# Combining expert results by diagonal matmuls tile by tile, with column norms, and a different gather and scatter distance

## The chip, the core and the metric

The program runs on one core of a Trainium2 chip. The metric is device time in microseconds (us). A core has TensorE (PE; PEld is its weight load), VectorE (DVE), ScalarE (ACT), GpSimd (POOL) and SyncE (SP); the last three start DMAs here. SBUF and PSUM have 128 partitions; PSUM has eight banks of 512 fp32 columns.

## The reference

One inference step of a two-layer trunk on 512 latent and 128 context tokens of width 1024, all in fp32. Layer 0 mixes by attention and retention, layer 1 by a convolution module; each is followed by a mixture of 32 experts of which every token uses two. Cut to the parts that the change touches:

```python
def rms_norm(x, g):
    y = x * lax.rsqrt(jnp.mean(x * x, axis=-1, keepdims=True) + EPS)
    return y * g

def conformer_conv(h, w_in, dw, dw_b, ln_g, ln_b, w_out):
    a, g = jnp.split(h @ w_in, 2, axis=-1)
    u = depthwise_conv(a * jax.nn.sigmoid(g), dw, dw_b)
    u = layer_norm(u, ln_g, ln_b)
    return jax.nn.silu(u) @ w_out

# grouped_expert_mlp, after rows are gathered by expert
def run(args):
    xb, e = args
    a, b = jnp.split(xb @ w_up[e], 2, axis=-1)
    return (jax.nn.silu(a) * b) @ w_down[e]
out_buf = lax.map(run, (x_buf, blk_exp)).reshape(P, D)
y = out_buf[dest].reshape(N, TOP_K, D) * top_w[..., None]
return jnp.sum(y, axis=1)          # x = x + gate * this
```

## The kernel before

Every engine has its own instruction stream, written out by hand. Semaphores named by `ev(...)` join them, and an engine waits in program order. There is no scheduler. Activations lie transposed: `xT` and `hT` hold 8 tiles of 128 features by 640 tokens, that is 5 token tiles of 128, the last being the context.

**Order of the work.** Layer 0 mixer, `project_out` (L589), norm, router and ranks, block loop over experts, combine; layer 1 norm, gated input (L1029), convolution taps (L1046 on PE, L1960 on DVE), layer norm, `project_out`, norm, router, block loop, combine, transposes out (L1080), output DMAs (L529).

**Block loop.** Tokens are sorted by expert into blocks of 64 rows. SP streams 3 MB of weights for each expert into 18 slots of 1 MB, six experts deep (`refill`, L473 and L476). POOL gathers a block's rows into one of four landing buffers (L2114) and scatters a result block to `y_rows` in HBM (L2119). Gathers go two blocks ahead, scatters four blocks behind; the last four scatters stand in a tail behind the loop, each after a wait for the one before it (`freed`). PE transposes rows (L930), multiplies up (L945) and down (L967); DVE takes landed rows (L1884) and the gated product; ACT copies a result block out of PSUM (L1388). The number of blocks is rounded up to a multiple of four.

**Combine.** POOL's `y_done` (L2177) lets ACT start five DMAs of 1 MB that bring each token tile's two results back, 128 tokens by 2 by 1024 (L1404). ACT scales the first by its weight (L1409), DVE adds the second times its weight (L1913), PE transposes (L1009), and DVE adds the result times the gate to `xT` (L1922).

**Norms.** `norm_sums` (L563, L564) or `norm_sum` (L571, L572) multiplies squares by a matrix of ones, so that every partition holds the sums of all 640 tokens. ACT takes the roots (L1178, L1179), DVE the reciprocals (L1485, L1486), DVE multiplies (L1456) and ACT scales and shifts (L1184). The layer norm does the same with L1054 and L1980.

Lines by name:

```python
    dve.wait_ge(ev("comb"), 2 * NT)     # all five tiles combined
    normed(2)                           # the norm ahead of layer 1
    link(dve.reciprocal(PS[:, 4, :], rs[:, 0:SAMPLE]))
```

## Time and profile before

| what | value |
|---|---|
| median of 3 runs | 1504.81 us (1500.93 to 1506.77) |
| the profiled execution's own time | 1506.75 us |
| its span in the profile | 1504.9 us |
| mean granted clock of TensorE | 0.929 of 2.4 GHz |
| busy PE / DVE / ACT / POOL | 83% / 40% / 21% / 20% |
| DMA, mean over the span | 214 GB/s |

Durations below are from the one profiled execution. 1.85 us of its time lie outside the span. PE's busy share is an average over stages with different limits, so the rows further down are read stage by stage. One fp32 matmul of the program appears as two PE instructions, a transpose as one. The two block loops run from 544.6 to 791.3 us and from 1213.5 to 1461.5 us. A timeline row reads: start, duration, engine, line, operation, output <- input, count, and in brackets the idle time before it and what ended that.

### The profile page before, as it was taken

Reading aid. Unit: us, or ns where it says so; the run is one execution under the profiler, and the core shown is the slowest. Engines: PE = TensorE matmul, PEld = TensorE weight load, DVE = VectorE, ACT = ScalarE, POOL = GpSimd, SP = SyncE. Lnnn points to the kernel's source line nnn. Section 1 sums busy time; section 2 is a strip of 40 time slices with the busy share of each in tenths; the row PEclk is TensorE's granted clock in tenths of the full one; section 3 lists DMA queues with packets and bytes.
Section 4 is the critical chain, followed back from the end, with each engine's and each line's share of the span. In section 5 each row is a group of like instructions: output and inputs, shape, how many; then the busy total and the mean of one; then the engine's idle time right before and its main releaser. Section 6 shows DMA issues by size and latency. Waiting matters only on the chain.

```text
span 1504.9 us, 20559 instructions
## 1 busy us (share of the span) xinstructions
PE 1254.5 (83%) x6795; PEld 779.2 (52%) x6796; DVE 601.5 (40%) x1364; ACT 310.2 (21%) x666; POOL 304.0 (20%) x703
## 2 busy tenths in 40 slices
PE   4999998888899669997771699999798679999764
PEld 3666775554467335543330367776475345555333
DVE  1211433765421632221111569999612622222115
ACT  3300145655300411111111300000311311111112
POOL 3000100300000024443332012240000034444420
PEclk9999999979999769999995699999899779999996
DMA  9575646300061169999999010100071279999965
GB/s 341 218 277 233 267 169 243 129 31 1 1 252 56 70 230 402 412 406 402 398 359 349 4 56 29 56 29 1 0 274 62 97 270 396 385 402 409 405 248 208
DMA packets 149091, 322.60 MB, mean 214 GB/s; under 512 B 16181, under 2 KB 49947, under 8 KB 142883
## 3 DMA queue, kind: packets, MB, share of 16 engines
q1 hardware_dynamic: 128432, 288.25, 50.3%
q0 software_dynamic: 12464, 21.91, 4.1%
q10 hardware_dynamic: 8131, 11.57, 2.1%
q8 instruction: 42, 0.69, 0.2%
q14 instruction: 22, 0.18, 0.0%
HBM read 312.41 MB, written 27.08 MB: 226 GB/s over the span
## 4 chain that ended last, share of the span: by engine, by line
PE 48%; DVE 16%; SPq 14%; DMA 8%; issue 7%; ACT 3%; POOL 2%; ACTq 1%; POOLq 0%; DVEq 0%
PE PS L589 10%; PE PS L638 8%; DVE arena L1960 8%; SPq L476 7%; PE PS L945 7%; SPq L473 5%; PE PS L967 3%; DMA ring<-in_moe_w_up 3%; PE PS L555 3%; PE PS L1029 2%; PE PS L812 2%; DMA arena<-y_rows 2%; DVE scratch L1456 2%; PE PS L1046 2%; PE PS L827 1%
## 5 line engine op out<-in xcount | busy, mean ns | idle before, releaser
L589 PE MATMUL PS<-arena,ring 128*128 128x320 f32 x512 | 144.1, 446 | 11.1 <-ACT arena L1435 7.4
L945 PE MATMUL PS<-arena 128*64 128x256 f32 x1152 | 134.7, 383 | 21.5 <-DMA arena<-in_moe_w_up 20.6
L1456 DVE TENSOR_TENSOR arena<-arena,PS 128x128 f32<-128x128 f32 (+1 forms) x85 | 27.1, 327 | 311.0 <-ACT arena L1377 304.7
L1960 DVE SCALAR_TENSOR_TENSOR arena<-arena,vecT 128x655 f32<-128x655 f32 x181 | 151.1, 908 | 0.0
L945 PE MATMUL PS<-ring,arena 128*64 128x256 f32 x1056 | 129.0, 395 | 23.2 <-DMA ring<-in_moe_w_up 21.6
L1029 PE MATMUL PS<-arena,ring 128*128 128x320 f32 x512 | 141.2, 437 | 8.3 <-ACT arena L1184 7.2
L638 PE MATMUL PS<-ring,arena 128*128 128x256 f32 (+1 forms) x640 | 140.3, 373 | 0.0
L589 PEld LDWEIGHTS PS<-arena,ring 128*128 128x128 f32 x512 | 100.6, 197 | 54.3 <-issue 15.7
L638 PEld LDWEIGHTS PS<-ring,arena 128*128 128x128 f32 x640 | 114.9, 190 | 26.5 <-issue 13.4
L1029 PEld LDWEIGHTS PS<-arena,ring 128*128 128x128 f32 x512 | 98.4, 193 | 49.9 <-issue 10.1
L945 PEld LDWEIGHTS PS<-arena 128*64 128x64 f32 x1152 | 80.2, 137 | 64.9 <-DMA arena<-in_moe_w_up 17.3
L945 PEld LDWEIGHTS PS<-ring,arena 128*64 128x64 f32 x1056 | 76.2, 141 | 66.3 <-DMA ring<-in_moe_w_up 19.1
L1377 ACT ACTIVATE arena<-PS 128x128 f32<-128x128 f32 x69 | 19.1, 277 | 275.6 <-PE PS L945 275.6
L2009 POOL TENSOR_SCALAR arena<-arena,modA,modT 128x128 f32<-128x128 f32 x24 | 10.7, 447 | 300.6 <-DVE arena L1456 300.6
L967 PE MATMUL PS<-arena 128*64 128x512 f32 x288 | 69.8, 605 | 1.5 <-ACT arena L1388 1.5
L2119 POOL DMA_INDIRECT y_rows<-arena,scatter_col x64 | 65.1, 1017 | 22.1 <-issue 22.1
L1388 ACT ACTIVATE arena<-PS 128x512 f32 x61 | 36.4, 597 | 147.3 <-PE PS L967 147.3
L1009 PE MATMUL PS<-cst,arena 128*128 128x128 f32 x80 | 19.4, 415 | 56.4 <-DVE arena L1913 43.1
L2114 POOL DMA_INDIRECT arena<-h_rows,gather_col x56 | 59.3, 1059 | 28.3 <-issue 28.3
L1743 DVE SCALAR_TENSOR_TENSOR xT<-PS,modT,xT 128x320 f32<-128x320 f32 (+2 forms) x48 | 18.2, 434 | 116.7 <-PE PS L589 116.7
L2105 POOL TENSOR_TENSOR pool_tick<-cst 128x1 f32<-128x1 f32 x128 | 24.7, 193 | 198.6 <-ACT arena L1388 193.3
L967 PE MATMUL PS<-ring,arena 128*64 128x512 f32 x264 | 63.9, 605 | 0.0
(317 smaller groups left out, 1633.9 us busy)
## 6 DMA issues: line engine op xcount, KB each, us to landing
ring<-in_moe_w_up SPq DMA_DIRECT2D x64, 1024.0 KB, 13.6
arena<-in_moe_w_up SPq DMA_DIRECT2D x64, 1024.0 KB, 13.7
ring<-in_ada_w SPq DMA_DIRECT2D x48, 1024.0 KB, 11.3
ring<-in_moe_w_down SPq DMA_DIRECT2D x32, 1024.0 KB, 15.6
arena<-in_moe_w_down SPq DMA_DIRECT2D x32, 1024.0 KB, 15.3
arena<-y_rows ACTq DMA_DIRECT2D x10, 1024.0 KB, 10.5
ring<-in_od_w_in SPq DMA_DIRECT2D x16, 512.0 KB, 6.2
ring<-in_ev_w_in SPq DMA_DIRECT2D x7, 1024.0 KB, 15.2
```

Of the source, the lines that this page charges most:

```text
L473: sp.dma_start(slot(s).rearrange("p (k n) -> p k n", k=4), src).then_inc(ring_full[s], 16)
L476: sp.dma_start(slot(s).rearrange("p (k n) -> p k n", k=2), src).then_inc(ring_full[s], 16)
L555: last = pe.matmul(PS[32 * c:32 * c + 32, 7, :], scT[:, j % KD, :], w[:, 512 * c:512 * c + 512], start=(j % KD == 0), stop=(j % KD == KD - 1))
L589: last = pe.matmul(PS[:, b + n, 0:SEG], w[:, k, c:c + P], src[:, tile(k), n * SEG:(n + 1) * SEG], start=(k == 0), stop=(k == KD - 1))
L638: last = pe.matmul(z_bank(i)[:, 0:n], hT[:, k, t * P:t * P + P], w[:, k, 0:n], start=(k == 0), stop=(k == KD - 1))
L945: last = pe.matmul(PS[i * BLK:(i + 1) * BLK, 0, 0:2 * P].rearrange("p (a n) -> p a n", a=2), xblk[:, k, :], w[:, k % 4, :, i * P:(i + 1) * P],
L967: last = pe.matmul(PS[c * BLK:(c + 1) * BLK, 2, :], hblk[:, i, :], w[:, i, c * 512:(c + 1) * 512], start=(i == 0), stop=(i == 1))
L1029: last = pe.matmul(PS[:, 2 * a + n, 0:SEG], w[:, k, a, :], hT[:, k, n * SEG:(n + 1) * SEG], start=(k == 0), stop=(k == KD - 1))
L1456: return dve.tensor_tensor(out, a, b, op)
L1960: dve.scalar_tensor_tensor(out=acc, in0=src, scalar=wc, in1=acc, op0=ALU.mult, op1=ALU.add).then_inc(ev("conv_v"), 1)
L2114: pool.indirect_dma_start(land[r], None, h_rows[:, :], bass.IndirectOffsetOnAxis(ap=col, axis=0), bounds_check=2 * T - 1, oob_is_err=False ...
L2119: pool.indirect_dma_start(y_rows[:, :], bass.IndirectOffsetOnAxis(ap=col, axis=0), yblk[r], None, bounds_check=2 * ROWS - 1, oob_is_err=Fa ...
```

## The change

The order in which each engine issues is written out in the source, so the listings below show it directly.

- Combine: PE multiplies both results of a tile by two diagonal matrices of the token weights (`wdiag`) and adds them in PSUM, which also transposes. ACT's scaling and DVE's sum are gone. DVE builds the ten diagonals ahead of the block loop. The context tile comes first.
- Norm ahead of layer 1: done tile by tile within the combine. Sums of squares are matmuls with one column of ones (`tile_sum`), root and reciprocal are 128x1, and a diagonal times ones spreads the result over all partitions (`spread`).
- The other two norms and the layer norm: one-column sums, root and reciprocal of 128x5, then one diagonal block and one spread.
- The transposes out at the end stand one tile behind the combine, from other PSUM banks.
- Gathers three blocks ahead, scatters two behind; within the POOL loop a gather stands ahead of the wait for the result block. The tail has two scatters. DVE takes landed rows behind the copy of `hblk`.
- SP waits for the five result tiles before it loads the first `od_w_in` slot.
- Some semaphores are merged under other names (`MODC`, `POOLSET`), with their counts.

PE, from the last block of layer 0's loop (L967, in the new file L981) to the first gated input of layer 1 (L1029, new L1086). Before:

```order
L967 MATMUL PS<-arena 64x512 x4
L1009 MATMUL PS<-cst,arena 128x128 x40
L563 MATMUL PS<-arena,cst 128x512
L564 MATMUL PS<-arena,cst 128x128
L563 MATMUL PS<-arena,cst 128x512
L564 MATMUL PS<-arena,cst 128x128
```

After, in the same place:

```order
L981 MATMUL PS<-arena 64x512 x4
L1027 MATMUL PS<-scratch,arena 128x128 x32
L1037 MATMUL PS<-cst,arena 128x1 x8
L1027 MATMUL PS<-scratch,arena 128x128 x16
L1037 MATMUL PS<-cst,arena 128x1 x8
L1046 MATMUL PS<-scratch,cst 128x128
L1027 MATMUL PS<-scratch,arena 128x128 x16
L1037 MATMUL PS<-cst,arena 128x1 x8
L1046 MATMUL PS<-scratch,cst 128x128
L1027 MATMUL PS<-scratch,arena 128x128 x16
L1037 MATMUL PS<-cst,arena 128x1 x8
L1046 MATMUL PS<-scratch,cst 128x128
```

Forty transposes of finished sums and then sixteen matmuls of sums of squares have become 80 diagonal matmuls (L1027) with the one-column sums (L1037) and spreads (L1046) between them.

DVE, in the same stretch. Before (L1913 sums two results, L1922 adds to `xT`, L1485 is the wide reciprocal):

```order
L1913 SCALAR_TENSOR_TENSOR arena<-arena,wtok 128x1024 x5
L1922 SCALAR_TENSOR_TENSOR xT<-PS,modT,xT 128x128 x40
L1485 RECIPROCAL PS<-scratch 128x512
L1486 RECIPROCAL PS<-scratch 128x128
```

After (L1994 adds to `xT`, L2002 and L2003 make a tile's diagonal, L1520 is the tile's product):

```order
L1994 SCALAR_TENSOR_TENSOR xT<-PS,modT,xT 128x128 x24
L2002 RECIPROCAL ss<-ss 128x1
L2003 TENSOR_SCALAR scratch<-cst,ss 128x128
L1994 SCALAR_TENSOR_TENSOR xT<-PS,modT,xT 128x128 x8
```

The sum of two results has gone, and the reciprocal of a tile stands behind the residual of the tile two later.

POOL, one iteration inside the block loop. Before (L2114 gathers, L2119 scatters, L2105 and L2109 are ticks):

```order
L2105 TENSOR_TENSOR pool_tick<-cst 128x1
L2154 ISA
L2154 COPY gather_col<-scratch 128x1
L2155 ISA
L2155 COPY scatter_col<-scratch 128x1
L2157 REGISTER_ALU
L2105 TENSOR_TENSOR pool_tick<-cst 128x1
L2114 DMA arena<-h_rows,gather_col 128x512
L2119 DMA y_rows<-arena,scatter_col 2560x512
```

After (L2209 gathers, L2214 scatters, L2200 and L2204 are ticks):

```order
L2200 TENSOR_TENSOR pool_tick<-cst 128x1
L2248 ISA
L2248 COPY gather_col<-scratch 128x1
L2249 ISA
L2249 COPY scatter_col<-scratch 128x1
L2251 REGISTER_ALU
L2200 TENSOR_TENSOR pool_tick<-cst 128x1
L2209 DMA arena<-h_rows,gather_col 128x512
L2200 TENSOR_TENSOR pool_tick<-cst 128x1
L2204 TENSOR_TENSOR pool_tick<-cst 128x1
L2214 DMA y_rows<-arena,scatter_col 2560x512
```

One more tick stands between gather and scatter, behind the wait for the result block. The diff, added lines alone (what they replace stands in the listing above):

```diff
+LAG = 2
+AHEAD = 3
...
+        wdiag = scratch[:, 0:2 * NT * P].rearrange("p (c t n) -> p c t n", c=2, t=NT)
+        rdiag = rs[:, :].rearrange("p (t n) -> p t n", t=NT)
+        xout = arena[:, 0:NT * D].rearrange("p (t n) -> p t n", t=NT)
...
+        TILES = [ST] + list(range(ST))
+        HN = {1: 0, 2: 2 * KD, 3: 2 * KD + NT}
+        ROOT = {1: 2, 2: 2, 3: 2 + NT + 1}
+        DIAG = {1: NT, 2: NT + 1, "ln": 2 * NT + 1, 3: 2 * NT + 2}
+        SPREAD = {1: 0, 2: 1, "ln": NT + 1, 3: NT + 2}
+        def cols(t):
+            return slice(t * P, t * P + P)
...
+                        if key == ("od_in", 0):
+                            for t in range(NT):
+                                sp.wait_ge(ring_full[SLOTS + t], back_full[int(last[0][6]), t])
...
+            def norm_sum(l):
+                pe.wait_ge(ev("sq_add"), (KD - 1) * (l + 1))
+                for t in range(NT):
+                    last = pe.matmul(PS[:, 4, t:t + 1], sq_sum[:, cols(t)], ones[:, 0:1], start=True, stop=True)
...
+                pe.wait_ge(ev("diag"), DIAG[2 * l + 1] + 1)
+                pe.matmul(PS[:, 4, :], ones, rs[:, 0:SAMPLE], start=True, stop=True)
+                pe.matmul(PS[:, 6, 0:CONTEXT], ones, rs[:, SAMPLE:T], start=True, stop=True) \
+                    .then_inc(ev("spread"), 1)
...
+                def combine(s):
+                    t = TILES[s]
+                    pe.wait_ge(ring_full[SLOTS + t], back_full[l, t])
+                    pe.wait_ge(ev("wdiag"), 2 * NT * (l + 1))
+                    for half in range(2):
+                        i = 2 * s + half
+                        if i >= 4:
+                            pe.wait_ge(ev("comb"), 2 * NT * l + i - 3)
+                        for m in range(4):
+                            c = (4 * half + m) * P
+                            for a in range(2):
+                                last = pe.matmul(quad(4 + i % 4)[:, m, :], ygat[:, t, a, c:c + P], wdiag[:, a, t, :],
+                                                 start=(a == 0), stop=(a == 1))
+                        last.then_inc(ev("comb_mm"), 1)
+                def tile_sum(s):
+                    pe.wait_ge(ev("squared"), KD + s + 1)
+                    if s >= 2:
+                        pe.wait_ge(ev("root"), ROOT[2] + s - 1)
+                    for k in range(KD):
+                        last = pe.matmul(PS[:, s % 2, 0:1], hT[:, k, cols(TILES[s])], ones[:, 0:1],
+                                         start=(k == 0), stop=(k == KD - 1))
+                    last.then_inc(ev("sumsq"), 1)
+                def spread(s):
+                    pe.wait_ge(ev("diag"), DIAG[2] + s + 1)
+                    if s >= 2:
+                        pe.wait_ge(ev("hn"), HN[2] + s - 1)
+                    pe.matmul(PS[:, 2 + s % 2, 0:P], ones, rdiag[:, s, :], start=True, stop=True) \
+                        .then_inc(ev("spread"), 1)
+                def turn_out(s):
+                    pe.wait_ge(ev("comb"), 2 * NT * l + 2 * s + 2)
+                    for half in range(2):
+                        i = 2 * s + half
+                        if i >= 4:
+                            pe.wait_ge(ev(("xt_v", "xt_a")[i % 2]), NT + (i - 4) // 2 + 1)
+                        for j in range(4):
+                            last = pe.transpose(quad(i % 4)[:, j, :], xT[:, 4 * half + j, cols(TILES[s])], ident)
+                        last.then_inc(ev("x_t"), 1)
+                for s in range(NT + 2):
+                    if s < NT:
+                        combine(s)
+                    if l == 0:
+                        if 1 <= s <= NT:
+                            tile_sum(s - 1)
+                        if s >= 2:
+                            spread(s - 2)
+                    elif 1 <= s <= NT:
+                        turn_out(s - 1)
...
+                pe.wait_ge(ev("ln_sq"), k + 1)
+                for t in range(NT):
+                    c = t * P if t < ST else CTX0
+                    last = pe.matmul(PS[:, 0, t:t + 1], cv2[:, k, c:c + P], ones[:, 0:1],
+                                     start=(k == 0 and t == 0), stop=(k == KD - 1 and t == NT - 1))
+                last.then_inc(ev("ln_mm"), 1)
+            pe.wait_ge(ev("diag"), DIAG["ln"] + 1)
+            pe.matmul(PS[:, 1, :], ones, rs[:, 0:SAMPLE], start=True, stop=True)
+            pe.matmul(PS[:, 2, 0:CONTEXT], ones, rs[:, SAMPLE:T], start=True, stop=True).then_inc(ev("spread"), 1)
...
+                    act.wait_ge(ev("hn"), HN[q] + 2 * k + 1)
+                    shift_scale(q, k)
+            def norm_tiles():
+                for s in range(NT + 1):
+                    if s < NT:
+                        act.wait_ge(ev("comb"), 2 * s + 2)
+                        act.activation(hT[:, :, cols(TILES[s])], xT[:, :, cols(TILES[s])], ACT.Square) \
+                            .then_inc(ev("squared"), 1)
+                    if s >= 1:
+                        act.wait_ge(ev("sumsq"), 1 + s)
+                        act.activation(ss[:, 1, s - 1:s], PS[:, (s - 1) % 2, 0:1], ACT.Sqrt, bias=eps, scale=1.0 / D) \
+                            .then_inc(ev("root"), 1)
+                act.wait_ge(ev("hn"), HN[2] + NT)
+                for k in range(KD):
+                    shift_scale(2, k)
...
+            def diagonals():
+                link(dve.reciprocal(ss[:, 0, 0:NT], ss[:, 1, 0:NT]))
+                tt(rdiag, bc(ident.unsqueeze(1), [P, NT, P]), bc(ss[:, 0, 0:NT].unsqueeze(2), [P, NT, P]),
+                   ALU.mult).then_inc(ev("diag"), 1)
...
+                dve.wait_ge(ev("root"), ROOT[q])
...
                     dve.wait_ge(ev(f"h_t{l}"), n + 2)
                     dve.wait_ge(ev(f"down_mm{l}"), n + 1)
                     dve.tensor_copy(hblk[:, :, :], PS[:, 1, 0:P].rearrange("p (i n) -> p i n", i=2)) \
                         .then_inc(ev(f"hblk_c{l}"), 1)
+                    take_landed(n + 2)
+                for c in range(2):
+                    for t in range(NT):
+                        dve.tensor_scalar(wdiag[:, c, t, :], ident, wtok[:, c, t:t + 1], None, ALU.mult) \
+                            .then_inc(ev("wdiag"), 1)
                 take_landed(0)
                 take_rows(0)
                 take_landed(1)
...
+                def residual(s):
+                    t = TILES[s]
+                    c = 0 if t < ST else 1
+                    for half in range(2):
+                        i = 2 * s + half
+                        dve.wait_ge(ev("comb_mm"), 2 * NT * l + i + 1)
+                        for m in range(4):
+                            k = 4 * half + m
+                            ins = dve.scalar_tensor_tensor(
+                                out=xT[:, k, cols(t)], in0=quad(4 + i % 4)[:, m, :], scalar=modT[:, l, 40 + k, c:c + 1],
+                                in1=xT[:, k, cols(t)], op0=ALU.mult, op1=ALU.add)
+                        ins.then_inc(ev("comb"), 1)
+                def tile_diag(s):
+                    dve.wait_ge(ev("root"), ROOT[2] + s + 1)
+                    link(dve.reciprocal(ss[:, 0, s:s + 1], ss[:, 1, s:s + 1]))
+                    dve.tensor_scalar(rdiag[:, s, :], ident, ss[:, 0, s:s + 1], None, ALU.mult) \
+                        .then_inc(ev("diag"), 1)
+                def normed_tile(s):
+                    dve.wait_ge(ev("spread"), SPREAD[2] + s + 1)
+                    tt(hT[:, :, cols(TILES[s])], xT[:, :, cols(TILES[s])],
+                       bc(PS[:, 2 + s % 2, 0:P].unsqueeze(1), [P, KD, P]), ALU.mult).then_inc(ev("hn"), 1)
+                def turned_out(s):
+                    dve.wait_ge(ev("x_t"), 1 + 2 * NT + 2 * s + 1)
+                    dve.tensor_copy(xout[:, TILES[s], 0:512], PS[:, (2 * s) % 4, :]).then_inc(ev("xt_v"), 1)
+                for s in range(NT + 3):
+                    if s < NT:
+                        residual(s)
+                    if l == 0:
+                        if 3 <= s:
+                            normed_tile(s - 3)
+                        if 2 <= s <= NT + 1:
+                            tile_diag(s - 2)
+                    elif 2 <= s <= NT + 1:
+                        turned_out(s - 2)
...
+            dve.wait_ge(ev("ln_sq"), KD + 1)
...
+            diagonals()
+            dve.wait_ge(ev("spread"), SPREAD["ln"] + 1)
...
+                tt(cvn[:, k, 0:SAMPLE], cv[:, k, 0:SAMPLE], PS[:, 1, :], ALU.mult).then_inc(ev("ln_d"), 1)
+                tt(cvn[:, k, SAMPLE:T], cv[:, k, CTX0:SPAN], PS[:, 2, 0:CONTEXT], ALU.mult).then_inc(ev("ln_d"), 1)
...
+                for b in range(AHEAD):
+                    gather(b, gather_at[:, b:b + 1])
...
+                    if b >= 1:
+                        pool.wait_ge(ev(f"x_taken{l}"), b)
+                    gather((b + AHEAD) % LAND, gather_at[:, b + AHEAD:b + AHEAD + 1])
...
+                        freed(b % LAND, b // LAND - 1)
+                    if b >= LAG:
+                        pool.wait_ge(ev(f"yblk_c{l}"), b - LAG + 2)
+                        scatter((b - LAG) % LAND, scatter_at[:, b - LAG:b - LAG + 1])
...
+                        pool.wait_ge(ev(f"x_taken{l}"), 4 * g + (2 * LAND + r))
+                        columns(r, g, 4 * g + (r + 1))
+                        gather((r + AHEAD) % LAND, gather_col[:, r:r + 1])
+                        pool.wait_ge(ev(f"yblk_c{l}"), 4 * g + (2 * LAND + r - LAG + 2))
+                        settle(4 * LAND + r)
+                        freed(r, g + 1)
+                        scatter((r - LAG) % LAND, scatter_col[:, r:r + 1])
+                for r in range(2):
+                    landed(r, laps + 2)
+                for r in range(LAG):
+                    pool.tensor_copy(scatter_col[:, r:r + 1], scatter_at[:, bass.ds(4 * laps + (2 * LAND + r - LAG), 1)]) \
+                        .then_inc(ev(f"column{l}"), 1)
+                for r in range(LAG):
+                    pool.wait_ge(ev(f"yblk_c{l}"), 4 * laps + (2 * LAND + r - LAG + 2))
+                    pool.wait_ge(ev(f"column{l}"), 4 * laps + LAG)
+                    settle(4 * LAND + r)
+                    scatter((r - LAG) % LAND, scatter_col[:, r:r + 1])
+                landed(2, laps + 2)
+                for r in range(2):
+                    pool.wait_ge(ev(f"y_sent{l}_{r}"), 32 * laps + 64)
+                    settle(4 * r + 2)
+                pool.tensor_tensor(pool_tick[:, 5 * LAND:], cst[:, 0:1], cst[:, 0:1], ALU.mult).then_inc(ev("y_done"), 1)
...
+            ctx_mod(2)
```

## Rows read from the trace of the kernel before

**Rows 1.** The page, part 4: shares of the chain that ended last.
```profile
PE 48%; DVE 16%; SPq 14%; DMA 8%; issue 7%; ACT 3%; POOL 2%; ACTq 1%; POOLq 0%; DVEq 0%
```

**Rows 2.** Windows, layer 0's loop: stretch, us, busy of PE, PEld, DVE, ACT, POOL, clock, DMA, GB/s.
```profile
655.00:800.00 145.00, 105.59 (x716) 52.12 (x712) 25.38 (x64) 16.03 (x49) 54.51 (x143) 0.99 1.02 383
```

**Rows 3.** Timeline, end of layer 0's block loop.
```profile
775.35 32.17 SPq L461 DMA_DIRECT2D ring<-in_od_w_in  x15
...
787.71 0.60 ACT L1388 ACTIVATE arena<-PS 128x512 f32 x1 [2.42 <-PE PS L967]
...
788.44 0.19 POOL L2105 TENSOR_TENSOR pool_tick<-cst 128x1 f32<-128x1 f32 x1 [4.51 <-ACT arena L1388]
...
790.66 0.60 ACT L1388 ACTIVATE arena<-PS 128x512 f32 x1 [2.36 <-PE PS L967]
...
792.35 0.19 POOL L2105 TENSOR_TENSOR pool_tick<-cst 128x1 f32<-128x1 f32 x1
...
804.46 1.01 POOL L2119 DMA_INDIRECT y_rows<-arena,scatter_col  x1 [0.51 <-issue]
...
809.27 0.19 POOL L2177 TENSOR_TENSOR pool_tick<-cst 128x1 f32<-128x1 f32 x1 [2.83 <-DMA y_rows<-arena,scatter_col]
...
817.41 1.15 ACT L1409 ACTIVATE arena<-arena,wtok 128x1024 f32<-128x1024 f32 x1 [26.06 <-DMA arena<-y_rows]
```

**Rows 4.** Timeline, from the last result tile to layer 1's first matmul.
```profile
828.76 1.28 DVE L1913 SCALAR_TENSOR_TENSOR arena<-arena,wtok 128x1024 f32<-128x1024 f32 x1 [1.20 <-ACT arena L1409]
829.97 10.42 DVE L1922 SCALAR_TENSOR_TENSOR xT<-PS,modT,xT 128x128 f32<-128x128 f32 x40
...
854.06 3.36 DVE L1485 RECIPROCAL PS<-scratch 128x512 f32<-128x512 f32 x1 [13.68 <-ACT scratch L1179]
...
859.24 3.14 ACT L1184 ACTIVATE arena<-arena,modT,modA 128x512 f32<-128x512 f32 x4 [5.28 <-DVE arena L1456]
...
860.14 2.47 PE L1029 MATMUL PS<-arena,ring 128*128 128x320 f32 x4 [7.17 <-ACT arena L1184]
```

**Rows 5.** Timeline, end of the program.
```profile
1465.38 0.19 POOL L2177 TENSOR_TENSOR pool_tick<-cst 128x1 f32<-128x1 f32 x1 [1.48 <-DMA y_rows<-arena,scatter_col]
...
1470.36 1.15 ACT L1409 ACTIVATE arena<-arena,wtok 128x1024 f32<-128x1024 f32 x1 [8.78 <-DMA arena<-y_rows]
...
1480.33 1.15 ACT L1409 ACTIVATE arena<-arena,wtok 128x1024 f32<-128x1024 f32 x1 [1.35 <-DMA arena<-y_rows]
...
1501.24 0.33 SPq L529 DMA_DIRECT2D out_y_prompt<-arena  x1
```

**Rows 6.** Chain of waits: 16 diagonal matmuls of the first stage (start, us).
```profile
32.29 3.77 PE PS L619 x32
```

**Rows 7.** Windows: the stretch of rows 6, all engines.
```profile
32.20:36.10 3.90, 3.90 (x38) 3.88 (x35) 0.00 (x0) 0.00 (x0) 0.00 (x0) 1.00 1.04 377
```

**Rows 8.** Windows, PE alone: the last transposes of the program (us, busy, clock, DMA, GB/s).
```profile
1498.50:1500.60 2.10, 2.04 (x17) 0.91 0.81 330
```

**Rows 9.** Timeline, weight loads of twelve transposes, at either clock.
```profile
1183.27 1.29 PEld L906 LDWEIGHTS PS<-cst,arena 128*128 128x128 f32 x12
...
1193.18 2.61 PEld L906 LDWEIGHTS PS<-cst,arena 128*128 128x128 f32 x12
```

**Rows 10.** Timeline, the norm ahead of layer 1's router.
```profile
1161.90 2.04 PE L571 MATMUL PS<-scratch,cst 128*128 128x512 f32 x2 [2.98 <-DVE scratch L1456]
...
1169.84 6.45 DVE L1456 TENSOR_TENSOR arena<-xT,PS 128x512 f32<-128x512 f32 x16
```

**Rows 11.** Timeline, the layer norm.
```profile
1070.41 9.09 PE L1054 MATMUL PS<-arena,cst 128*128 128x328 f32 x32 [1.95 <-ACT arena L1427]
...
1080.53 3.35 DVE L1980 RECIPROCAL scratch<-scratch 128x512 f32<-128x512 f32 x1 [5.37 <-ACT scratch L1431]
...
1084.90 6.53 DVE L1456 TENSOR_TENSOR arena<-arena,scratch 128x512 f32<-128x512 f32 x16
```

**Rows 12.** The page, part 6: DMA issues of the gated input's weights.
```profile
ring<-in_od_w_in SPq DMA_DIRECT2D x16, 512.0 KB, 6.2
```

220 lines of the change are left out of this document (63 added, 157 removed).

## Prediction, made before the changed kernel ran

> **What bounds the kernel now.** I read the page's chain shares first, then a table of windows by stage, then the timeline at the four places that the change touches. The chain [rows 1] shows PE at 48%, DVE at 16%, and 22% on SP's queue and DMA: no single engine. Inside the block loop the DMA engines are the limit: between 655 and 800 us the DMA share is 1.02 at 383 GB/s, while PE is busy for 105.6 of 145 us [rows 2]. The loop ends when the weights have arrived, whatever order rows are gathered in. What can shrink is the serial work around the loops, where each engine waits for the one before it.
>
> The largest such stretch lies behind layer 0's loop. The last result block leaves PSUM at 791.3 (790.66 plus 0.60), but the gathering back is released only at 809.3, since the scatters trail by four blocks and each tail scatter waits for the one before; meanwhile SP has been loading `od_w_in` since 775.35. The first result tile arrives at 817.41 [rows 3]. The last addition of two results starts at 828.76, 40 residual additions take 10.42 us, then come sums of squares, roots and a reciprocal of 3.36 us, and layer 1's first matmul starts at 860.14 [rows 4]. Behind layer 1's loop there is the same chain with fewer scatters left: release 1465.4, first tile 1470.36, last tile 1480.33, last output DMA 1501.24 [rows 5], end of the span 1504.9.
>
> **The change part by part.** Prices first. An fp32 matmul is two PE instructions. Diagonal matmuls of just this shape exist: 32 instructions in 3.77 us [rows 6], with the clock at full 2.4 GHz [rows 7]. So a token tile's combine, 16 matmuls, costs 3.8 us at the upper level. A one-column matmul does not exist in this trace. Its floor is its two weight loads: twelve loads take 1.29 us at the upper level and 2.61 at the lower, 0.107 and 0.217 each [rows 9]. Its ceiling is a full 128-column matmul, 0.118 an instruction [rows 6], at the lower level twice that. I take 0.118 where PE is warm, being close to both ends: 16 instructions, 1.9 us, for a tile's sum.
>
> The Trainium skill ("TensorE: Matmul & The Clock Gate", LDWEIGHTS) puts a weight load at its columns divided by 1.2 GHz, 107 ns for 128, whatever the clock. The trace agrees at the upper level and not at the lower, where it has 217 ns [rows 9]; by the page's figure each of the two cold norms below would be 1.1 us shorter.
>
> *Ten diagonals ahead of the loop* stand on DVE while the first gather is under way. I cost them at nothing; at most 10 times 0.3 us, if that cover were gone.
>
> *POOL's tail in layer 0.* A loop iteration takes 3.9 us when nothing is missing (788.44 to 792.35); with one tick more I take 4.2. Block 31's result is out at 788.3 (787.71 plus 0.60). Its scatter ends at 790.2. Two iterations follow, 798.6, then two scatters of 1.0 with their ticks and column copies, 4.3 together, then landing and ticks, 2.4: release at 805.3 against 809.3 [rows 3]. The gathers back no longer share the queues with `od_w_in`. Then the first tile takes as long as in layer 1, 5.0 us from release [rows 5], not 8.1 [rows 3]: 810.3 instead of 817.4. Bounds of this term: 0 to 10 us earlier.
>
> *Combine and norm of layer 0.* PE is now the pace, since tiles land every 2.5 us (1470.36 to 1480.33 is four intervals) [rows 5] and PE needs more. PE comes cold, so the first combine costs between 3.8 and 6.9 (32 times 0.217); I take 5.8: 816.1. Then combine 1 819.9, sum 0 821.8, combine 2 825.6, sum 1 and a spread (0.4) 827.9, combine 3 831.7, sum 2 and spread 834.0, combine 4 837.8. The tail is a chain through all engines: half a tile's residual 1.1 (0.26 each [rows 4]) to 838.9; DVE's queued product of tile 1 (1.3, like the 128x1024 operation of 1.28 [rows 4]) and a diagonal 0.5 to 840.7; spread 841.1; sum 4 843.0, root 0.3; spread 3, product 3 and diagonal 4 to 845.2; spread 845.6, product 4 846.9; then 0.9 from ACT's first shift to the first matmul, as 859.24 to 860.14 [rows 4]: 847.8. That is 12.4 us earlier than 860.14. In this sum 6.4 us of DVE additions, ACT's scaling and the 4.3 us of reciprocals go; late next is PE. The `od_w_in` loads now start when the last tile is in, about 820; 6.2 us to landing [rows 12] makes 827, twenty before they are needed. If that cover were gone they would cost their excess alone.
>
> *The other two norms.* Before, 7.9 us from the first sum (1161.90) to the first product (1169.84) [rows 10]. After: ten one-column instructions at the lower level 2.2, root 0.3, reciprocal 0.25, diagonal block 128x640 0.85 (1.28 scaled), spread 2.5 (2.04 for 512 columns [rows 10], a quarter more for 128), hand-off 0.1: 6.2. Gain 1.75 each, 3.5 together. Bounds 0 and 8.
>
> *The layer norm.* Before, 14.5 us from 1070.41 to 1084.90, of which 4.4 are reciprocals [rows 11]. After: 80 one-column instructions, 9.0 (8.6 by weight loads, 9.4 by full matmuls), root, reciprocal and diagonal 1.4, spread at the upper level 1.3, hand-off 0.1: 11.8. Gain 2.7. Bounds: a loss of 6.5, if the sums run at 0.217, and a gain of 4.
>
> *The end.* The first tile lands as before, 1470.3: the scatter distance matters little where results come singly. Combine 0 1476.1, combine 1 1479.9, turn 0 (eight transposes at 0.12, 17 in 2.04 us [rows 8]) 1480.9, and 4.8 for each further tile: combine 4 at 1494.3. Residual 1.1, DVE's copy of tile 2 that frees the bank 0.7, last transposes 1.0, copy 0.7: 1497.8. Its DMA takes the 3.7 us that lay between 1501.24 [rows 5] and the span's end: 1501.5. Gain 3.4.
>
> The Trainium skill says in the same page (Part 4: PE-mode transpose) that the full clock does not engage for transposes. Here it does: nothing but transposes runs at the very end, with the granted clock at 0.91 [rows 8]. By the page the old end would have stayed slow, and the four turns would cost 4 us more in the new one.
>
> *Gather and scatter distance inside the loop*: nothing, since weights bound it [rows 2]; a gather is now issued before a result block is waited for, and a scatter only after; a landed tick now stands behind that wait, and the extra block of distance makes up for it. Bounds: 3 us either way per loop.
>
> Sum: 12.4 + 3.5 + 2.7 + 3.4 = 22.0. From the profiled execution's own 1506.75 that is 1484.8; it lies 1.9 above the median shown, so 1482.8 on the scale of the runs.
>
> **The rivals.**
> *The start of the gathering back does not move.* From block 31's result on POOL still issues two gathers and five scatters, with more ticks. Then the first tile comes at 817.4 and layer 0 gains 5.3: 1489.9. For it: issues of about 1 us each do the tail's timing [rows 3], not only the waits between them.
> *One-column sums cost double.* 0.217 an instruction everywhere: 8.8 more in the layer norm (80 instructions), 8.8 more in the five tile sums: 1500.4. For it: such matmuls hardly use the array, and nothing here has measured them. Against it: weight loads at 0.107 [rows 9].
> *TensorE stays warm across the shorter gaps.* The norms' cold start [rows 10] goes, 2.4 each, and so does that of the first matmuls of the next stage (four in 2.47 at 860.14 [rows 4]), 2: 1476.
> *Slower: the combine stays at 1.2 GHz.* PE now does 80 matmuls where 40 transposes stood, and they follow the tiles' arrival after 20 us of idling. At 0.217 an instruction a combine costs 6.9 and a sum 3.5. Combine 4 then ends at 857.1 and the first matmul of layer 1 starts at 870.8, 10.7 late; the end comes 14.0 late; with the other gains the time is 1523. It decides when more than half of the combine's work runs at the lower level, as 22.0 is about half of the 40.5 between the two cases. Against it: PE has work without a gap from the second tile on.
>
> **How the numbers follow.** Forecast 0.58; warm PE 0.12; no earlier gathering 0.12; double sums 0.12; slower 0.06. The time is the forecast's, 1482.8. The range runs from 1473 (below the warm case) to 1497 (beyond the case without earlier gathering, and most of the way to doubled sums) and leaves out about two in ten. The forecast's own range is 1476 to 1490. Half a per cent is 7.5 us, about what the runs can tell. Faster takes the first three, 0.82, and a part of the double sums, 0.05: 0.87. The same 0.07, slower 0.06.
>
> **What would show it.** Right: the five result DMAs are released near 805 and the first tile is used near 810; diagonal matmuls at 0.12 an instruction from the second tile on, granted clock 1.0; layer 1's first matmul 57 us or less behind the last result block instead of 69; no 128x512 reciprocal; block loops as long as before. Wrong: a loop that is longer or shorter by more than 3 us; one-column matmuls at 0.2; a clock of 0.5 beyond the first tile; release still at 18 us behind the last block; a gated input that waits for `od_w_in`.

## The result, and the profile after

| | before | after |
|---|---|---|
| median of the runs | 1505.62 us (1500.93 to 1506.77) | 1496.16 us (1492.5 to 1496.46) |
| the profiled execution | 1506.75 us | 1496.46 us |
| its span | 1504.9 us | 1494.6 us |
| mean granted clock of TensorE | 0.929 | 0.936 |

The ratio of after to before is 0.9938, 95% interval 0.9911 to 0.9965: 9.5 us faster by the medians, where 22.0 had been forecast. In a second measurement, on another chip, it was 0.9944 (0.9931 to 0.9957).

The chain of the profile after reads, against [rows 1]:

```profile
PE 48%; issue 16%; DVE 15%; POOL 7%; SPq 5%; DMA 5%; ACT 3%; ACTq 1%; POOLq 1%; DVEq 0%
```

The chain now runs partly through GpSimd, where it ran through SP's queue. That is a change of name more than of length: the loops last as long as before, within about 1 us (table below).

**The tail of layer 0's loop**, against [rows 3]. Timeline, end of layer 0's loop; the last result block goes out at 793.06.

```profile
792.46 0.60 ACT L1458 ACTIVATE arena<-PS 128x512 f32 x1 [2.36 <-PE PS L981]
...
805.06 0.19 POOL L2278 TENSOR_TENSOR pool_tick<-cst 128x1 f32<-128x1 f32 x1
...
821.61 23.32 SPq L480 DMA_DIRECT2D ring<-in_od_w_in  x16
```

The release comes 12.0 us behind the last result block, 18.0 before. The gated input's weights are loaded from 821.61 on instead of 775.35.

**Combine and norm of layer 0**, against [rows 4]. Timeline, PE, from the first result tile to layer 1's first matmul.

```profile
810.08 9.15 PE L1027 MATMUL PS<-scratch,arena 128*128 128x128 f32 x64 [17.90 <-DMA arena<-y_rows]
819.07 1.84 PE L1037 MATMUL PS<-cst,arena 128*128 128x1 f32 x16
820.78 3.82 PE L1027 MATMUL PS<-scratch,arena 128*128 128x128 f32 x32
...
833.33 5.37 PE L1027 MATMUL PS<-scratch,arena 128*128 128x128 f32 x32
...
842.06 3.41 PE L1037 MATMUL PS<-cst,arena 128*128 128x1 f32 x16
...
850.82 1.41 PE L1086 MATMUL PS<-arena,ring 128*128 128x320 f32 x2 [2.21 <-issue]
```

The first two combines take 9.15 us and the third 3.82, as worked out, and the fourth takes 3.74. A tile's sum costs 1.84 us, 0.115 an instruction. But the fifth combine stretches to 5.37, and the last sum takes 3.41. The clock shows why. Windows of PE: stretch, us, busy, clock, DMA share, GB/s.

```profile
828.00:832.00 4.00, 3.94 (x37) 1.00 1.15 346
...
834.00:838.00 4.00, 4.00 (x24) 0.57 0.98 285
...
842.00:846.00 4.00, 4.00 (x20) 0.50 1.13 342
```

**The layer norm**, against [rows 11]. Timeline of PE, then its windows.

```profile
1061.09 15.52 PE L1130 MATMUL PS<-cst,arena 128*128 128x1 f32 x80 [1.95 <-ACT arena L1493]
1078.05 2.08 PE L1134 MATMUL PS<-scratch,cst 128*128 128x512 f32 x2 [1.44 <-DVE scratch L1520]
```

```profile
1061.10:1063.00 1.90, 1.90 (x17) 0.98 0.00 0
1063.00:1065.00 2.00, 2.00 (x12) 0.50 0.00 0
...
1070.00:1076.60 6.60, 6.60 (x31) 0.50 0.00 0
```

Eighty one-column instructions take 15.52 us, 0.194 each, and TensorE is busy all the time. Two us into this busy stretch the granted clock falls from 0.98 to 0.50, and stays there.

**The norm ahead of the router of layer 1**, against [rows 10], and what follows.

```profile
1156.80 1.25 PE L582 MATMUL PS<-cst,scratch 128*128 128x1 f32 x10 [2.98 <-DVE scratch L1520]
1159.56 2.08 PE L585 MATMUL PS<-scratch,cst 128*128 128x512 f32 x2 [1.51 <-DVE scratch L1520]
...
1162.10 2.28 DVE L1520 TENSOR_TENSOR arena<-xT,PS 128x512 f32<-128x512 f32 x5 [2.59 <-PE PS L586]
```

From the first sum to the first product it is 5.3 us, 7.9 before.

**The end**, against [rows 5]: release, first two combines, ScalarE's last copy out of PSUM.

```profile
1458.83 0.19 POOL L2278 TENSOR_TENSOR pool_tick<-cst 128x1 f32<-128x1 f32 x1
...
1464.03 9.82 PE L1027 MATMUL PS<-scratch,arena 128*128 128x128 f32 x64 [9.80 <-DMA arena<-y_rows]
...
1490.21 0.60 ACT L1506 ACTIVATE arena<-PS 128x512 f32<-128x512 f32 x1 [1.50 <-PE PS L1057]
```

Stage by stage, from the timelines of all profiled executions (us; each column is one execution). The work of the first row is the same in all of them, and it still varies by 7 us, so the spans of two profiles are not compared, only their stages. The release is the start of GpSimd's `y_done` tick; a loop ends with the last result block's copy out of PSUM.

| stage | before | after | wait only | no wait | old distances | 100 columns | all wide |
|---|---|---|---|---|---|---|---|
| start to the first norm's sums | 492.8 | 493.7 | 489.8 | 494.6 | 492.6 | 496.8 | 494.8 |
| norm, router, ranks, layer 0 | 51.8 | 52.1 | 52.3 | 52.0 | 51.2 | 52.4 | 49.0 |
| loop, layer 0 | 246.7 | 247.3 | 246.2 | 248.1 | 246.2 | 248.3 | 246.3 |
| last block to release | 18.0 | 12.0 | 11.3 | 14.8 | 11.4 | 12.0 | 11.4 |
| release to PE's first combining work | 10.7 | 5.0 | 7.6 | 6.9 | 5.1 | 5.3 | 5.1 |
| combine and norm, to layer 1 | 40.2 | 40.7 | 39.8 | 44.9 | 38.6 | 38.5 | 37.7 |
| conv and layer norm, to projection | 226.8 | 231.8 | 226.6 | 231.8 | 231.8 | 224.6 | 224.7 |
| projection, to norm | 75.0 | 74.2 | 74.9 | 74.5 | 74.6 | 74.7 | 74.8 |
| norm, router, ranks, layer 1 | 51.6 | 51.4 | 52.6 | 51.1 | 51.7 | 51.5 | 48.0 |
| loop, layer 1 | 248.0 | 246.9 | 246.6 | 247.3 | 246.5 | 247.9 | 248.0 |
| end | 43.4 | 39.5 | 43.4 | 39.6 | 39.8 | 39.2 | 39.3 |

### The profile page after: what moved, and what is told of

Read it like the earlier page. It is cut to its first block, busy times and chain, and to the rows that moved or that the text cites. A ratio compares the mean times of both kernels' runs of the same rounds, so it can differ in the third digit from the quotient of the medians.

```text
span 1494.6 us, 21245 instructions
## 1 busy us (share of the span) xinstructions
PE 1291.7 (86%) x7165; PEld 825.5 (55%) x7166; DVE 587.8 (39%) x1371; ACT 296.3 (20%) x653; POOL 313.9 (21%) x745
## 4 chain that ended last, share of the span: by engine, by line
PE 48%; issue 16%; DVE 15%; POOL 7%; SPq 5%; DMA 5%; ACT 3%; ACTq 1%; POOLq 1%; DVEq 0%
PE PS L603 10%; PE PS L652 8%; DVE arena L2059 8%; PE PS L959 4%; POOL arena L2209 3%; PE PS L1027 3%; PE PS L574 3%; PE PS L1086 2%; SPq L495 2%; PE PS L826 2%; PE PS L981 2%; SPq L492 2%; DVE scratch L1520 2%; PE PS L1103 2%; DVE arena L1520 2%
## 5 line engine op out<-in xcount | busy, mean ns | idle before, releaser
L1086 PE MATMUL PS<-arena,ring 128*128 128x320 f32 x512 | 141.2, 437 | 3.3 <-issue 2.2
L1086 PEld LDWEIGHTS PS<-arena,ring 128*128 128x128 f32 x512 | 98.2, 192 | 45.2 <-issue 5.5
L1954 DVE COPY arena<-arena 128x512 f32 (+1 forms) x73 | 31.6, 433 | 180.2 <-POOL pool_tick L2204 180.2
L1520 DVE TENSOR_TENSOR arena<-arena,PS 128x128 f32<-128x128 f32 (+1 forms) x101 | 33.5, 350 | 112.8 <-ACT arena L1447 103.7
L2200 POOL TENSOR_TENSOR pool_tick<-cst 128x1 f32<-128x1 f32 x176 | 37.4, 212 | 170.3 <-ACT arena L1458 162.3
L981 PE MATMUL PS<-arena 128*64 128x512 f32 x288 | 69.7, 605 | 1.5 <-ACT arena L1458 1.5
L2104 POOL TENSOR_SCALAR arena<-arena,modA,modT 128x128 f32<-128x128 f32 x24 | 10.7, 450 | 275.6 <-DVE arena L1520 275.6
L2291 POOL TENSOR_SCALAR arena<-cst,vecT 128x128 f32<-128x128 f32 x51 | 41.5, 831 | 125.6 <-PE PS L1103 125.6
L2214 POOL DMA_INDIRECT y_rows<-arena,scatter_col x60 | 61.1, 1018 | 28.6 <-issue 28.6
L1027 PE MATMUL PS<-scratch,arena 128*128 128x128 f32 x320 | 43.1, 301 | 27.7 <-DMA arena<-y_rows 27.7
L2209 POOL DMA_INDIRECT arena<-h_rows,gather_col x56 | 59.1, 1056 | 24.8 <-issue 24.8
## 6 DMA issues: line engine op xcount, KB each, us to landing
ring<-in_ada_w SPq DMA_DIRECT2D x48, 1024.0 KB, 11.1
```

Source lines behind the costliest of these rows:

```text
L981: last = pe.matmul(PS[c * BLK:(c + 1) * BLK, 2, :], hblk[:, i, :], w[:, i, c * 512:(c + 1) * 512], start=(i == 0), stop=(i == 1))
L1027: last = pe.matmul(quad(4 + i % 4)[:, m, :], ygat[:, t, a, c:c + P], wdiag[:, a, t, :], start=(a == 0), stop=(a == 1))
L1086: last = pe.matmul(PS[:, 2 * a + n, 0:SEG], w[:, k, a, :], hT[:, k, n * SEG:(n + 1) * SEG], start=(k == 0), stop=(k == KD - 1))
L1520: return dve.tensor_tensor(out, a, b, op)
L2209: pool.indirect_dma_start(land[r], None, h_rows[:, :], bass.IndirectOffsetOnAxis(ap=col, axis=0), bounds_check=2 * T - 1, oob_is_err=False ...
L2214: pool.indirect_dma_start(y_rows[:, :], bass.IndirectOffsetOnAxis(ap=col, axis=0), yblk[r], None, bounds_check=2 * ROWS - 1, oob_is_err=Fa ...
```

## The experiments

Each ratio is to the kernel before, timed on the same chip. The kernels fall into four groups: what shortens the tail, the layer norm, the router stages, and the combinations.

### What shortens the tail of layer 0

The first run was to show what the distances bring.

```
-AHEAD = 3, LAG = 2: gathers three ahead, scatters two behind
+gathers two ahead, scatters four behind; POOL's and DVE's order, ticks as before
```

> The changed kernel with the gather and scatter distances (and GpSimd's order and ticks) of before: gathers two ahead, scatters four behind; combine, norms and the later load of the gated input kept. Theory A (the distances only shorten layer 0's tail): release 18 us behind the last result block instead of 12, loops as long as before (246.7 and 248), so 6 us slower than the changed kernel: 1502.5. Rival 1 (the new distances cost the loops something, since VectorE now waits for landed rows 180 us over the loops instead of 12): one or both loops 2 us or more shorter, net under 3 slower. Rival 2 (the gain came from taking the weights of the gated input away from the gathering back): release at 12 to 13 here too, no difference.

Measured: 0.9890 (0.9874 to 0.9907), 1491.26 us. The release comes 11.4 us behind the last result block with the old distances. So rival 2 held in its release, though not in its "no difference": the new distances do not shorten the tail here, and where the theory expected a loss of 6 us the ratio is 7 to 8 us better than the changed kernel's. Both kernels share the later load of the gated input's weights. The next run makes that edit alone.

```
 sp.wait_ge(ev(f"down_mm{last[0][6]}"), expert_done(e))
+if key == ("od_in", 0):
+    for t in range(NT):
+        sp.wait_ge(ring_full[SLOTS + t], back_full[int(last[0][6]), t])
```

> The kernel before with one edit of the change alone: SyncE loads the gated input's weights only when layer 0's result tiles have been gathered back. The run with the old distances has shown the short release (11.4 us behind the last result block) without the new distances, so theory: this wait alone is what shortens the tail. Then release 12 us behind the last result block instead of 18, the first tile 5 behind it instead of 8, layer 1's first matmul 7 to 9 us earlier, the whole 7 to 8 us faster than before (ratio 0.995). Rival (what counts is that the gated weights were needed early): the gated input waits for its weights and nothing is gained. Rival 2 (GpSimd's order or the new combine shortened it): release stays at 18.

Measured: 0.9931 (0.9917 to 0.9944), 1495.25 us. These three lines bring as much as the whole change. Release 11.3 us behind the last block, first tile 5.0 behind that, layer 1's first matmul 58.7 behind the last block instead of 68.9. GpSimd's last rows show the mechanism; first before, then with the wait alone.

```profile
796.35 0.33 POOL L2109 TENSOR_TENSOR pool_tick<-cst 128x1 f32<-128x1 f32 x2 [1.87 <-DMA y_rows<-arena,scatter_col]
...
799.92 0.19 POOL L2109 TENSOR_TENSOR pool_tick<-cst 128x1 f32<-128x1 f32 x1 [1.18 <-DMA y_rows<-arena,scatter_col]
...
803.22 0.19 POOL L2109 TENSOR_TENSOR pool_tick<-cst 128x1 f32<-128x1 f32 x1 [1.05 <-DMA y_rows<-arena,scatter_col]
```

```profile
791.58 0.35 POOL L2112 TENSOR_TENSOR pool_tick<-cst 128x1 f32<-128x1 f32 x2
...
793.99 0.22 POOL L2112 TENSOR_TENSOR pool_tick<-cst 128x1 f32<-128x1 f32 x1
...
799.68 0.19 POOL L2180 TENSOR_TENSOR pool_tick<-cst 128x1 f32<-128x1 f32 x1 [0.93 <-DMA y_rows<-arena,scatter_col]
```

Before, each scatter of the tail is waited for, five waits of 0.79 to 2.83 us and 7.7 together. With the wait on SyncE the earlier scatter has always landed, and only the last one is waited for, 0.93 us. The difference, 6.8 us, accounts for the shorter release (6.7). The same windows of both kernels (us; PE, PEld, DVE, ACT, POOL; clock, DMA share, GB/s), before first:

```profile
791.20:799.20 8.00, 0.00 (x0) 0.00 (x0) 0.00 (x0) 0.15 (x2) 4.44 (x13) 0.78 1.01 305
```

```profile
791.20:799.20 8.00, 0.00 (x0) 0.00 (x0) 0.00 (x0) 0.00 (x0) 5.72 (x18) 0.58 0.08 28
```

The DMA engines were full with 8 MB of weights, first used at 860.14. Now they carry the scatters alone. The Trainium skill ("DMA: Bandwidth & Descriptors", Issuing engines are not separate DMA queues) says that transfers of all issuing engines run on the same 16 DMA engines and interleave; the trace agrees: without the loads four of the five waits are gone, and the fifth is 0.93 us instead of 2.83.

The counterpart: the changed kernel with those three lines taken out.

> The changed kernel without that wait: the gated input's weights are loaded as early as before, the new distances and the new combine stay. Theory (the wait shortens the tail): release 16 to 18 us behind the last result block instead of 12, the first tile 8 behind it instead of 5, 7 to 9 us slower than the changed kernel. Theory of the prediction (the distances shorten it): release stays at 12, and only the first tile comes up to 3 us later.

Measured: 0.9969 (0.9953 to 0.9985), 1502.90 us, against 0.9944 for the changed kernel on the same chip. Release 14.8 us behind the last block, combining work starts 21.7 behind it instead of 17.0. Without the wait the new distances do shorten the release, from 18.0 to 14.8; with it they have nothing left to shorten. The theory's release, 16 to 18, and its 7 to 9 us were both too much: by the ratios the loss is 3.8 us, by the medians 5.6. The nine executions spread over 9.5 us, and the profiled one is the slowest of them, so its stages show more than the median lost.

```
 the wait alone, and besides AHEAD = 3, LAG = 2 with the new order of POOL and DVE
```

> The kernel before with the wait of SyncE for the gathered tiles (as run before) and, besides, the new gather and scatter distances with GpSimd's and VectorE's new order; combine and norms as before. Theory (the distances cost the loops 1.5 us in layer 0 and 0.5 in layer 1, and give the tail nothing once the wait is there): 2 us slower than the wait alone, ratio 0.9945 against 0.9931, release 12 us behind the last result block. Rival (they still help where the old combine follows): release at 9 or less, 2 us faster than the wait alone.

Measured: 0.9942 (0.9921 to 0.9963), 1497.41 us; release 12.0 us behind the last block. The rival fell. The intervals of the two overlap, so a loss by the distances is not shown by this pair. It is in the profiles: seven executions with the old distances have 246.2 to 247.0 us in layer 0's loop (mean 246.5), nine with the new ones 246.3 to 248.3 (mean 247.5). Layer 1's loop has 247.0 and 247.2, which is within its spread. With the 0.7 us in the tail that is nearly 2 us, against the new distances. By its runs the old-distance kernel is 7 to 8 us faster than the changed one, and its profile has 2.1 less in the combines. That is not the distances' doing: four kernels that share the changed kernel's code up to the end of this stage, new distances included (those of the layer norm, below), took 38.0 to 38.6 us there, where the changed kernel's two executions took 40.7 and 40.9. The fifth combine of the one with wide sums:

```profile
834.23 3.74 PE L1027 MATMUL PS<-scratch,arena 128*128 128x128 f32 x32
```

So the same code ran this stage at either clock, and where the rest of the 7 to 8 us lies stays open.

```
+if key == ("od_in", 0):
+    sp.wait_ge(ev("y_done"), 1)
```

> The kernel before, with the gated input's weights held back only until layer 0's scatters are done (GpSimd's last tick), not until the result tiles are back. Theory (the loads slow the scatters, which share the DMA engines with them, and separately the gathering back): release 11.5 us behind the last result block as with the full wait, but the first tile is used 9 to 10 behind the release instead of 7.5, and the later tiles late too: it keeps 6.5 of the 10 us of the full wait, ratio 0.9955. Rival (only the scatters were slowed): as fast as the full wait, 0.993. Rival (only the gathering back was slowed): no faster than before.

Measured: 0.9944 (0.9925 to 0.9963), 1497.01 us. Release 11.3 behind the last block; the middle (last block to layer 1's first matmul) takes 62.5 us, 68.9 before and 58.7 with the full wait: 6.4 of the 10.2. So both are slowed by the weights, the scatters by 6.7 us (18.0 to 11.3) and what follows the release by 3.8 (62.5 to 58.7). The times alone do not decide it, as the interval holds the full wait's ratio too; the stages do. ScalarE's rows show the second part, the shorter wait first, then the full one: tiles 2.86 apart instead of 2.5.

```profile
809.46 1.15 ACT L1411 ACTIVATE arena<-arena,wtok 128x1024 f32<-128x1024 f32 x1 [17.67 <-DMA arena<-y_rows]
812.32 1.15 ACT L1411 ACTIVATE arena<-arena,wtok 128x1024 f32<-128x1024 f32 x1 [1.71 <-DMA arena<-y_rows]
```

```profile
804.72 1.15 ACT L1412 ACTIVATE arena<-arena,wtok 128x1024 f32<-128x1024 f32 x1 [16.29 <-DMA arena<-y_rows]
807.28 1.15 ACT L1412 ACTIVATE arena<-arena,wtok 128x1024 f32<-128x1024 f32 x1 [1.42 <-DMA arena<-y_rows]
```

The changed kernel once more, as the baseline on the second chip:

> The changed kernel once more, unaltered, as the baseline on the same chip. Expected: ratio 0.994 to the kernel before, from first to last stage as in its first profile within 1 us, except where TensorE's clock comes up at another moment.

Measured: 0.9944 (0.9931 to 0.9957), 1497.32 us; every stage from the first sums on within 0.5 us of the first profile.

### The layer norm

```
-pe.matmul(PS[:, 0, t:t + 1], cv2[:, k, c:c + P], ones[:, 0:1], ...)   # per tile, roots 128x5
+ln_sums(cv2, k, 0, "ln_sq", k + 1)      # ones x squares, wide roots and reciprocals
```

> The changed kernel with the layer norm alone put back as it was: wide sums of squares, wide roots, wide reciprocals. Theory A (the one-column sums let TensorE's granted clock fall, and cost 15.5 us where wide ones cost 9.1): from first sum to first product 14.5 us instead of 19.5, the whole program 5 us faster than the changed kernel, 1491.5 against its profiled 1496.5. Theory B (what was lost is lost in the gaps between stages, and any other form of the layer norm only moves it): within 1.5 us of the changed kernel, and a cold clock in the output projection behind it.

Measured: 0.9905 (0.9889 to 0.9922), 1494.07 us. The stage takes 226.7 us, 226.8 before and 231.8 after. That is theory A's 5 us; the projection behind it takes 75.0 us, 75.0 before.

```
+pe.matmul(PS[:, 3, 0:256], ones, cv2[:, k, 0:256], start=True, stop=True)   # per k
```

> The changed kernel with a superfluous 256-column matmul (two instructions) behind every ten one-column instructions of the layer norm's sums, into an unused bank: its result is not read. Theory A (the clock falls because one-column matmuls give TensorE too little work): the clock stays at 1.0, 80 one-column instructions cost 0.117 each, 9.4 us, the eight extra matmuls 0.43 each, 3.5 (256 of the 655 columns that cost 1.14 before): 12.9 us instead of 15.5, although work is added. Rival (a one-column matmul costs 0.19 whatever surrounds it): 15.5 and 3.5 or more, 19 to 22 us, the program 3.5 to 7 slower than the changed kernel.

Measured: 1499.68 us in a single run, which says little of the whole; the stage takes 237.4 us, 5.6 more than the changed kernel's. Timeline and windows of PE:

```profile
1056.94 1.25 PE L1130 MATMUL PS<-cst,arena 128*128 128x1 f32 x10 [1.94 <-ACT arena L1494]
1058.05 0.68 PE L1133 MATMUL PS<-arena,cst 128*128 128x256 f32 x2
1058.56 1.89 PE L1130 MATMUL PS<-cst,arena 128*128 128x1 f32 x10
1060.31 1.20 PE L1133 MATMUL PS<-arena,cst 128*128 128x256 f32 x2
1061.31 2.13 PE L1130 MATMUL PS<-cst,arena 128*128 128x1 f32 x10
```

```profile
1057.00:1059.00 2.00, 2.00 (x16) 0.95 0.00 0
1059.00:1061.00 2.00, 2.00 (x9) 0.50 0.00 0
```

The expectation of theory A was wrong: the extra matmuls did not hold the clock. The rival had the stage's loss right (3.5 to 7), but not its reason, a fixed price: ten one-column instructions took 1.25 us at 1.0 and 2.13 at 0.5. They have two prices, 0.125 and 0.213, and the clock chooses. Whether the single column or the weight loads in a row lower it was still open.

```
-PS[:, 0, t:t + 1], cv2[:, k, c:c + P], ones[:, 0:1]
+PS[:, 0, t * 100:t * 100 + 100], cv2[:, k, c:c + P], ones[:, 0:100]
```

> The changed kernel with the layer norm's sums made 100 columns wide instead of one (the same 80 instructions and weight loads; the 99 further columns repeat the first and are not read). Theory A (the clock falls because one-column matmuls leave the array idle): the clock stays at 1.0, 80 instructions at 0.118, 9.4 us where one-column ones took 15.5; the whole 6 us faster than the changed kernel. Rival (weight loads one after another are what lowers the clock): it falls as before, 80 instructions at 0.2 or more, 15.5 us or longer, nothing gained. The last experiment, in which 256 columns every ten instructions did not hold the clock, speaks for this rival or for a mix that was too thin.

Measured: 0.9879 (0.9862 to 0.9896), 1487.12 us, 10 faster than the changed kernel on the same chip. The stage takes 224.6 us, 7.2 less. Another 2.3 us of the profiles' difference lie in the combines, ahead of the edit and in the same code.

```profile
1063.92 9.14 PE L1131 MATMUL PS<-cst,arena 128*128 128x100 f32 x80 [1.95 <-ACT arena L1494]
1074.51 1.13 PE L1135 MATMUL PS<-scratch,cst 128*128 128x512 f32 x2 [1.44 <-DVE scratch L1521]
```

```profile
1065.00:1067.00 2.00, 2.00 (x21) 1.00 0.00 0
...
1071.00:1073.00 2.00, 2.00 (x19) 1.00 0.00 0
```

The same 80 instructions and weight loads, with a hundred times the columns: 9.14 us instead of 15.52. The spread behind them takes 1.13 instead of 2.08. So weight loads in a row do not lower the clock by themselves; these one-column matmuls do. Nor is it the gap of 1.95 us ahead of the sums, which stands here as well. From the first sum to the first product it is 11.97 us, 14.49 before: 2.5 of the forecast's 2.7. It is no chance of one execution either: the stage took 231.8 us in all five profiles with these one-column sums and 224.4 to 224.7 in all three with 100 columns.

```
+tt(cv2[:, 4, :], cv2[:, 4, :], cv2[:, k, :], ALU.add)    # DVE, k = 5, 6, 7; PE sums k = 0 to 4
```

> The changed kernel, but VectorE adds the squares of row groups 5, 6 and 7 onto group 4 (three additions of 0.82 us, once its centring is done), and TensorE sums five groups instead of eight: 50 one-column instructions for 80. Theory A: the first four groups run at 0.12 to 0.19 (4.7 to 7.8 us from 1061.1), the last is free when VectorE is done, at 1066.3 + 2.5 = 1068.8, and takes 1.2 to 2.2: sums end at 1070 to 1071 instead of 1076.6, the program 6 us faster than the changed kernel: 1490.5, about level with the wide sums. Rival (all 50 at 0.217 from the start): end at 1072, 4.6 faster. If the sums were not on the path: no gain at all.

Measured: 0.9875 (0.9859 to 0.9892), 1489.68 us; the stage takes 226.5 us, 5.2 less than the changed kernel's 231.8. Theory A's gain was put at 6; the clock fell here too, and 40 instructions took 6.45 us.

### The router stages

```
 norm_sum, between the sums and the wait for the diagonals:
+pe.matmul(PS[:, 7, 0:512], ones, sq_sum[:, 0:512], start=True, stop=True)
```

> The changed kernel with a superfluous 512-column matmul (two instructions, into an unused bank, not read) behind the one-column sums of each of the two norms, in the gap in which TensorE waits 1.4 us for the diagonals. Theory (the shorter sums leave TensorE less busy ahead of the router, so that the spread and the router's matmuls, 10.7 to 11.0 us instead of 9.8 to 10.4, run at 1.2 GHz for longer): the clock is up at the spread, which takes 1.4 instead of 2.6, and the router's matmuls take 9.8: 1 to 2 us faster per layer, 2 to 4 in all. Rival (the clock comes up at the same moment whatever stands there): nothing gained, and up to 0.7 us lost per norm where the extra matmul outlasts the gap.

Measured: 0.9905 (0.9887 to 0.9924), 1491.22 us. In layer 0 norm, router and ranks take 48.4 us instead of 52.1. In layer 1 they take 51.6, as before: the clock fell at the spread, as in the changed kernel. Timeline of PE at layer 0's router, with the extra matmul, and without it (the second profile of the changed kernel):

```profile
497.84 0.53 PE L589 MATMUL PS<-scratch,cst 128*128 128x128 f32 x2
500.14 8.77 PE L892 MATMUL PS<-arena,wr 128*36 128x320 f32 x32 [1.78 <-ACT arena L1226]
```

```profile
497.27 0.63 PE L586 MATMUL PS<-scratch,cst 128*128 128x128 f32 x2
499.69 11.13 PE L889 MATMUL PS<-arena,wr 128*36 128x320 f32 x32 [1.78 <-ACT arena L1223]
```

Half of the theory: added work in front of a stage brought it up earlier in one layer and not in the other.

### The combinations

Old distances, 100 columns in the layer norm and in the tile sums:

> The changed kernel with the distances of before, and with 100-column sums in the layer norm and in the sums tile by tile behind layer 0's loop. Theory: what these two edits gave by themselves adds up, 7.0 (distances) and 6.5 (layer norm), and the tile sums keep the clock up during the combines, 1 to 2 us: 13 to 15 us faster than the changed kernel, ratio 0.985 or less to the kernel before. Rival (the sums between the combines are too few to matter): 12 to 13.

Measured: 0.9856 (0.9835 to 0.9876), 1484.32 us: 13 us below the changed kernel by the ratio, where theory and rival meet, so it does not decide between them. The middle takes 54.3 us, 55.1 with the old distances alone; all tile sums take 1.93 us and the combines behind the first two 3.74 to 3.76.

With 100 columns and the extra matmul in the norms too:

> The kernel of the third run of this group's theories together: as the one with old distances and 100-column sums in layer norm and tile sums, and besides 100-column sums and the superfluous 512-column matmul in the two norms. Theory: 2 to 4 us faster than the one without them, ratio 0.983. Rival: equal within 1 us.

Measured: 0.9806 (0.9788 to 0.9824), 1476.88 us. Norm, router and ranks take 49.0 and 48.0 us, 3.2 and 3.6 less than in the run before. Now layer 1's spread is fast, 1.12 us for 512 columns. Layer 0's is not, 2.04, but its router's matmuls take 8.78 us instead of 11.12. Layer 1:

```profile
1143.68 1.33 PE L584 MATMUL PS<-cst,scratch 128*128 128x100 f32 x10 [2.98 <-DVE scratch L1524]
1144.85 1.05 PE L587 MATMUL PS<-scratch,cst 128*128 128x512 f32 x2
1146.52 1.12 PE L589 MATMUL PS<-scratch,cst 128*128 128x512 f32 x2 [0.63 <-DVE scratch L1524]
```

And with the squares of two groups added by VectorE:

> The widened kernel (old distances, 100-column sums everywhere, the extra matmul in the norms' gap), and in the layer norm VectorE adds the squares of groups 6 and 7 onto group 5, so that TensorE sums six groups: 60 instructions. Theory: with the clock held at 1.0 the sums end with VectorE's last addition (1.7 us behind its centring) and one group, 7.7 us from the first sum instead of 9.14: 1.4 us faster than without, ratio 0.980. Rival (with a pause in the sums the clock falls again before the spread): no gain or a loss of up to 1.

Measured: 0.9800 (0.9783 to 0.9818), 1475.44 us; the stage is as long as without it, 224.7. The rival described it. The sums end 8.0 us from their start instead of 9.1, but PE paused in them, and the spread ran cold:

```profile
1056.67 1.36 PE L1137 MATMUL PS<-cst,arena 128*128 128x100 f32 x10 [0.80 <-DVE arena L1527]
1059.47 2.07 PE L1141 MATMUL PS<-scratch,cst 128*128 128x512 f32 x2 [1.44 <-DVE scratch L1527]
```

The last two are level by their intervals. Both beat the kernel before by 29 to 30 us and the changed kernel by some 20.

## Why the prediction was wrong in size, point by point

- *Layer norm, "Gain 2.7".* This step failed: from first sum to first product 14.49 us became 19.50, a loss of 5.0. Of the missing 12 us it is 7.7. The price, "0.118 where PE is warm", was right; the sentence assumed that PE stays warm, since it is busy all the time. It was warm at the start, and within 2 us of one-column matmuls the clock fell (0.194 measured). The Trainium skill ("TensorE: Matmul & The Clock Gate", Why this matters for your kernels) names idle gaps between bursts as what loses the clock; by that this stretch without a gap would have stayed at 1.00, and the trace does not agree. The prediction's bound, a loss of 6.5, held it. The rival of doubled sums came true here, and in the tile sums only for the last (3.41 us for 1.84). The run with 100 columns gives 2.5 of the 2.7, so the term's other prices held.
- *The other two norms, "3.5 together".* 1.6 and 2.6 measured to the first product, but the stage behind them, router and ranks, gave 2.0 and 2.5 back. The forecast had put that stage at nothing: it counted what the norm saves and not at which clock the work behind it runs. In layer 0 the router's matmuls took 11.16 us for 10.32, and the ranks behind them 1.1 more. The runs with the extra matmul, with and without 100 columns, show that such a loss is the clock's. That the narrow sums cause it is not shown. The kernel with the wait alone has this stage as before, and there too the sums ran fast, the first product came 1.15 us sooner, and the stage was no shorter: 52.3 and 52.6 us against 51.8 and 51.6. Its sums, against 2.04 us before:

```profile
489.80 1.10 PE L574 MATMUL PS<-scratch,cst 128*128 128x512 f32 x2 [2.98 <-DVE scratch L1459]
```

- *POOL's tail, "release at 805.3 against 809.3".* The release came 12.0 us behind the last block, 14 forecast, and the first tile 5.0 behind that, as forecast. That both stand at the forecast's very times, 805.06 and 810.08, is luck: the last block went out 1.8 us later. The cause was wrong. The forecast gave the earlier release to the distances and used the later load of `od_w_in` only for the first tile. The runs with the wait alone and with the old distances show that the load does both, and the distances nothing once it is moved. Rival 1, with the start not moving, fell. Its reason holds only for the tail without the loads: there the issues and ticks set the length, 11.3 us with four scatters in the tail and 12.0 with two.
- *Combine and norm of layer 0, "12.4 us earlier".* 11.1 measured, the first matmul 57.8 us behind the last block (the sum's own 847.8 is 12.3 earlier than 860.14). The order and prices held to the fourth combine. Then the clock fell twice, 834 to 838 and from 842 on; with old distances and 100 columns it held through the sums, and the middle was 54.3 us, 14.6 below before. But 10.2 of the 11.1 come with the wait alone: diagonals and tiles by themselves brought 1 us here, and about 3 in the four kernels of the layer norm, where the fifth combine ran fast (55.2 to 55.8 us).
- *The end, "Gain 3.4".* 3.9, right, and the place where the new combine pays most by itself.
- *Transposes at the end* ran at 0.13 an instruction (eight in 1.04 us), near the forecast's 0.12 from [rows 8], and at a granted clock of 1.00 in the last eight (1.06 us). By the section of the Trainium skill that the prediction cites there ("TensorE: Matmul & The Clock Gate", Part 4: PE-mode transpose) they would have been slow; the trace does not agree.
- *The loops, "nothing".* Right within its bounds: 0.6 longer and 1.1 shorter in this profile, 1.1 and 0.2 longer in the mean over all.
- *The slower rival*, a combine at 1.2 GHz: 1.00 from 816 to 834, so it did not come.
- *The rival of a warm TensorE* came true in part: layer 1's ten one-column sums took 1.25 us, where 2.2 had been put, but the spread took 2.08.
- *The doubled sums' price.* The rival's 8.8 us counts from 0.107 an instruction; from the forecast's own 9.0 and 1.9 it is 8.4 and 7.9.

By the terms: 22.0, less 7.7 (layer norm), 3.7 (norms with what follows), 1.3 (middle), and 0.9 of a later start, plus 0.5 (end) and 1.3 (loops and projection), is 10.2; the profiles differ by 10.3.

## What to carry to other kernels

Ask of every large load what small, serial transfers run while it is under way: eight megabytes that are first used 69 us behind the last result block cost 10 us here, and one wait on the issuing engine gets them back. A matmul that is made narrow saves nothing if its weight load sets its price, and can cost the clock of all that stands behind it: compare the granted clock at the end of such a stretch, not at its start, and widen the output where PSUM has room. Before a stage's time is put down to an edit, look at the same stage in kernels that the edit does not touch: TensorE's clock alone moved it by 1 to 3 us here. When a change bundles several edits, run each alone: here one brought 10 us, the new combine at the end 4, one cost 5 and one about 2.

## What the runs showed of the hardware

TensorE's granted clock fell from 0.98 to 0.50 two us into 15.5 us in which it was never idle, with one-column matmuls, and stayed at 1.00 for the same instructions with 100 columns. A 256-column pair after every ten did not hold it. Scatters of GpSimd's queue, 1 us to issue, were waited for 0.79 to 2.83 us each beside weight loads at 305 to 343 GB/s; without the loads only the last was, 0.93 us. Five result tiles of 1 MB came 2.86 us apart beside the loads (3.8 for the last) and 2.5 without.
